# A plain first step in the first FFN, with the modulation sums divided between TensorE and VectorE

## The chip, the cores and the metric
The kernel runs on one core of one Trainium2 chip. The metric is device time of one execution in microseconds (us). A core has five engines with programs of their own: TensorE (PE in the profile), VectorE (DVE), ScalarE (ACT), GpSimd (POOL) and SyncE (SP), which here issues all DMAs. They wait for each other through semaphores only.

## The reference, cut to what matters
One layer of a streaming encoder on x of 1024 tokens by 1024 features, all in fp32: a SwiGLU FFN, a token mixer, a second FFN, each behind an RMS norm that is modulated from a vector c. The change touches the beginning of the first FFN.

```python
c_act = silu(c)
mod = c_act @ w_ada + b_ada            # 1024 x 9216, nine rows of 1024
(sh1, sc1, gt1, ...) = split(mod, 9)
h = rms_normalize(x) * (1 + sc1) + sh1
g, u = split(h @ w_ffn1_in, 2)         # 1024 x 5632
x = x + 0.5 * gt1 * (silu(g) * u) @ w_ffn1_out
```

## The kernel before, in words
**Products in three parts.** An fp32 operand is cut into a high part (rounded by ACT, `cut_hi`) and a low part (the difference, by VectorE or GpSimd, `cut_lo`). PE then does three fast matmuls, high by high, high by low and low by high, each 128x128 weights by 512 columns (L1271 to L1273).

**Halved steps.** The first FFN's input product runs in 11 steps. A step makes 512 of the 5632 columns for all 1024 tokens. It splits the inner dimension and the tokens in halves (b11, b12, b21, b22 are the quarters of the transposed h; b11 and b21 belong to the first 512 tokens, b12 and b22 to the last) and, by Winograd's form of Strassen's scheme, makes seven products instead of eight: p1 = b11, p2 = b21, p6 = t2, p7 = t3, p5 = t1, p3 = b22, p4 = t4, in this order. The t are sums of quarters: t1 = b12 - b11, t2 = b22 - t1, t3 = b22 - b12, t4 = b21 - t2. Every product exists for two groups g of weights (gate and up columns), and each of these 14 parts takes 4 x 3 = 12 matmuls, 168 a step. The weights are summed in the same manner by GpSimd (`sum1` to `sum4`), cut by ACT and GpSimd and held in a ring of seven slots, m and m + 7 in one slot. VectorE adds products from PSUM (u2, u3, c22, c12, c21), multiplies by the silu that ACT makes (a11, a22, a21, a12) and makes four sums s1 to s4 (`sums123`, `sum4`); SP stores seven operands a step for the output product.

**The start.** `Start` prepares this. SP loads pieces of w_ada for the first two rows of the modulation (8 pieces, k = 0 to 7, 1 MiB each, ring of four), the eight tiles of x (128 tokens, 0.5 MiB each, two behind each of the first four pieces), the weights of step 0 (2 MiB, ahead of the last piece) and the last piece. VectorE multiplies each piece by its 128 values of c_act and adds it to `ada_lead_acc` (L618, L621; the last in two halves, L628). PE sums the accumulator over partitions with a column of ones (L604), which gives scale and shift as columns in PSUM, half by half. Meanwhile ACT squares and scales each tile, GpSimd makes 1/rms, PE turns it (eight transposes, L596), and VectorE and ACT keep the low and the high half of it (L631, L581). Then h is modulated (b11, b21 by VectorE at L650, b12, b22 by ACT at L658), cut, and the t are made, before and during step 0. Steps 1 to 8 also carry the remaining 7 rows of the modulation: eight "rest pieces" a step, summed by VectorE into PSUM (L670, L673). A piece waits on SP for the place of the piece two before it.

**What sets the order.** All queues are written out by hand in `ffn`: one block for each engine, every engine strictly in its own order. On ACT `keep_s1` copies each p1 out of PSUM, because p2 adds on the same bank. On VectorE a step is: `hidden11`, rest 0 and 1, u2 of both groups, rest 2, u3 of both, rest 3, c22 of both, a22, rest 4, c12, a21, the three sums, rest 5, c21, a12, s4, rest 6 and 7. In step 0 the low parts of t1 and t4 stand between u2, u3 and c22.

## Time and profile before
| | us |
|---|---|
| median of 3 runs (2015.03 to 2016.78) | 2015.71 |
| profiled execution | 2015.16 |
| its span, first to last instruction | 2013.4 |
| PE busy | 1901.3 |
| VectorE, GpSimd, ACT busy | 1174.6, 893.3, 761.5 |
| mean granted TensorE clock | 0.985 |

The span is the profiler's, from the first instruction to the last; the execution's own time has 1.8 us around it. A busy PE is an engine with work in its pipe: matmuls start every 0.23 us and are shown 0.39 us long. Times of rows are counted from the span's start. Where a row of the timeline has x4, four instructions are merged and the second number is their length together.

### The profile page before, as it was taken

To read this page: it belongs to the slowest core of one execution; us is meant where nothing else is said; L and a number is where in the kernel's file an instruction comes from. 1 tells how busy PE (TensorE), PEld (TensorE's weight loads), DVE (VectorE), ACT (ScalarE), POOL (GpSimd) and SP (SyncE) were. 2 spreads that over 40 slices of the span, in tenths; PEclk is the share of its full clock that TensorE was granted. 3 is DMA by queue.
4 is the path that set the end of the run, shared out by engine and by line. 5 is a ranking of instruction groups with operands and counts; after the bars stand their busy time and mean duration, and the time that the engine had idled before them with its cause. 6 is when DMAs were issued, how large, how long until landed. Compare 5 with 4: busy or idle time off the path is not lost. (4 is left out here: it accounts for less than half of the span.)

```text
span 2013.4 us, 25362 instructions
## 1 busy us (share of the span) xinstructions
PE 1901.3 (94%) x9280; PEld 1556.2 (77%) x9280; DVE 1174.6 (58%) x1680; ACT 761.5 (38%) x1390; POOL 893.3 (44%) x642
## 2 busy tenths in 40 slices
PE   4599999999999969999999999998999999999997
PEld 3488888888888857777778887777788888888886
DVE  5867666754778780544434465559434444448777
ACT  5533222322444441444431554344323323334444
POOL 4887778766000052100012133478878778710002
PEclk9899999999999979999999999999999999999998
DMA  7155656542886301311112112433223323159652
GB/s 297 49 184 173 202 174 210 185 159 83 320 274 198 115 23 42 127 43 43 43 37 76 51 42 84 156 117 104 95 96 114 105 87 123 63 207 344 206 189 84
DMA packets 208106, 267.93 MB, mean 133 GB/s; under 512 B 14302, under 2 KB 125170, under 8 KB 206450
## 3 DMA queue, kind: packets, MB, share of 16 engines
q1 hardware_dynamic: 207986, 266.34, 39.4%
q8 instruction: 74, 1.21, 0.3%
q14 instruction: 46, 0.38, 0.1%
HBM read 211.16 MB, written 53.03 MB: 131 GB/s over the span
## 5 line engine op out<-in xcount | busy, mean ns | idle before, releaser
L420 POOL TENSOR_TENSOR ffn_ring_b<-ffn_raw_in,ffn_ring_b 128x512 fp32r<-128x512 f32 x174 | 246.8, 1424 | 144.8 <-ACT ffn_ring_b L415 144.8
L832 PE MATMUL bank<-ffn_w_hi,ffn_a_hi 128*128 128x512 f32 x616 | 240.0, 390 | 1.2 <-DVE ffn_w_lo L816 1.2
L834 PE MATMUL bank<-ffn_w_hi,ffn_a_lo 128*128 128x512 f32 x616 | 239.7, 389 | 0.0
L833 PE MATMUL bank<-ffn_w_lo,ffn_a_hi 128*128 128x512 f32 x616 | 239.7, 389 | 0.0
L1545 POOL TENSOR_TENSOR mx_w_lo<-mx_raw_w,mx_w_hi 128x1024 fp32r<-128x1024 f32 x28 | 67.5, 2420 | 364.4 <-ACT mx_w_hi L1369 297.6
L415 ACT CAST ffn_ring_b<-ffn_raw_in 128x512 fp32r<-128x512 f32 x174 | 107.9, 621 | 300.2 <-PE bank L1273 284.3
L108 POOL TENSOR_SCALAR rms<-rms 128x1 f32<-128x1 f32 x24 | 14.0, 583 | 443.8 <-ACT ffn_junk L102 430.0
L805 ACT CAST ffn_a_hi<-ffn_a_stage 128x512 fp32r<-128x512 f32 x154 | 95.6, 621 | 201.9 <-PE bank L834 197.6
L1094 DVE TENSOR_TENSOR ffn_u<-bank,ffn_u 128x512 f32<-128x512 f32 x111 | 76.4, 688 | 163.1 <-PE bank L1273 163.1
L1271 PE MATMUL bank<-h_hi,ffn_ring_a_hi 128*128 128x512 f32 x356 | 142.4, 400 | 27.8 <-ACT ffn_g L1022 18.5
L816 DVE TENSOR_TENSOR ffn_a_lo<-ffn_a_stage,ffn_a_hi 128x512 fp32r<-128x512 f32 x154 | 106.4, 691 | 74.1 <-ACT ffn_a_hi L805 74.0
L1271 PE MATMUL bank<-t_hi,ffn_ring_b 128*128 128x512 f32 x356 | 139.8, 393 | 3.3 <-DVE t_lo L287 3.3
L1272 PE MATMUL bank<-h_lo,ffn_ring_a_hi 128*128 128x512 f32 x356 | 140.5, 395 | 0.0
L1273 PE MATMUL bank<-h_hi,ffn_ring_a_lo 128*128 128x512 f32 x356 | 140.4, 394 | 0.0
L1272 PE MATMUL bank<-t_lo,ffn_ring_b 128*128 128x512 f32 x356 | 138.6, 389 | 0.0
L1273 PE MATMUL bank<-t_hi,ffn_ring_b 128*128 128x512 f32 x356 | 138.5, 389 | 0.0
L1094 DVE TENSOR_TENSOR ffn_g<-bank,ffn_g 128x512 f32<-128x512 f32 x111 | 76.3, 687 | 105.2 <-PE bank L1273 105.2
L1271 PE MATMUL bank<-h_hi,ffn_ring_b 128*128 128x512 f32 x348 | 135.5, 389 | 1.8 <-issue 1.8
L832 PEld LDWEIGHTS bank<-ffn_w_hi,ffn_a_hi 128*128 128x128 f32 x616 | 115.6, 188 | 26.8 <-DVE ffn_w_lo L816 1.5
L1273 PE MATMUL bank<-h_hi,ffn_ring_b 128*128 128x512 f32 x348 | 135.4, 389 | 0.0
L1272 PE MATMUL bank<-h_lo,ffn_ring_b 128*128 128x512 f32 x348 | 135.4, 389 | 0.0
L834 PEld LDWEIGHTS bank<-ffn_w_hi,ffn_a_lo 128*128 128x128 f32 x616 | 115.6, 188 | 24.3
(337 smaller groups left out, 4676.9 us busy)
## 6 DMA issues: line engine op xcount, KB each, us to landing
ffn_raw_in<-in_w_ffn_in SPq DMA_DIRECT2D x88, 512.0 KB, 6.0
ffn_a_stage<-hidden SPq DMA_DIRECT2D x154, 256.0 KB, 3.4
ffn_w_stage<-in_w_ffn_out SPq DMA_DIRECT2D x132, 256.0 KB, 3.1
ada_rest<-in_w_ada SPq DMA_DIRECT2D x64, 448.0 KB, 4.1
hidden<-ffn_u SPq DMA_DIRECT2D x88, 256.0 KB, 2.0
hidden<-ffn_g SPq DMA_DIRECT2D x66, 256.0 KB, 2.0
mx_raw_w<-in_w_mix_in SPq DMA_DIRECT2D x28, 512.0 KB, 3.9
ada_ring<-in_w_ada SPq DMA_DIRECT2D x8, 1024.0 KB, 12.0
```

Of the source, the lines that this page charges most:

```text
L415: act.copy(self.hi(q), self.source(b, m)).then_inc(self.hi_done, 1)
L420: pool.tensor_tensor(self.lo(q), self.source(b, m), self.hi(q).bitcast(F32), ALU.subtract)\
L805: act.copy(self.op(self.buf.a_hi, n), self.a_source(n)).then_inc(self.hi_done, 1)
L816: dve.tensor_tensor(self.op(lo, n), source, self.op(hi, n).bitcast(F32), ALU.subtract)\
L832: pe.matmul(dst, a_hi, w_hi, start=first, stop=False, skip_group_check=True)
L833: pe.matmul(dst, a_hi, w_lo, start=False, stop=False, skip_group_check=True)
L834: mm = pe.matmul(dst, a_lo, w_hi, start=False, stop=True, skip_group_check=True)
L1094: dve.tensor_tensor(dst, core.bank[:, bank_of(b, p) + g, :], src, ALU.add).then_inc(made, 1)
L1271: pe.matmul(dst, w_hi, h_hi, start=(fresh and k == 0), stop=False, skip_group_check=True)
L1272: pe.matmul(dst, w_hi, h_lo, start=False, stop=False, skip_group_check=True)
L1273: mm = pe.matmul(dst, w_lo, h_hi, start=False, stop=(k == 3), skip_group_check=True)
L1545: pool.tensor_tensor(lo, raw_w[:, slot, :], hi.bitcast(F32), ALU.subtract).then_inc(w_lo_done[slot], 1)
```

## The change
The first FFN's step 0 becomes plain. It has eight products instead of seven (k = 0 to 7 of the inner dimension, 512 tokens at a time, weights as loaded, not summed): 2 halves x 8 k x 4 column tiles x 3 = 192 matmuls. The first half needs tokens 0 to 511 alone (tiles 0 to 3). Tiles 4 to 7 are squared, scaled, turned and kept during it: PE turns tile 4 behind k = 1, tile 5 behind k = 2, tile 6 behind k = 4, tile 7 behind k = 5. The second half takes b12 and b22 themselves, whose low parts stand for that time where the high parts of t4 and t1 come later.

All parts of the first weights are cut by ACT and VectorE. GpSimd begins with the weight sums of step 1. The t operands are cut after the plain step's own, and t1, t3, t4 and the halved b22 in step 1. The results of the plain step need no sums from PSUM: silu, one multiplication each, then the sums s1 to s4.

The modulation: PE sums pieces 0 and 2 directly from the ring (each 16 matmuls of 128x128 by one column of c_act, into the banks in which it adds VectorE's accumulator at the end); VectorE sums pieces 1, 3, 4, 5, 6 and 7. The ring has six places. The order on SP is tile 0, piece 0, tile 1, piece 1, ..., tile 3, piece 3, pieces 4 to 7, the first weights, tiles 4 to 7; then, after the sums of columns, the weights of step 1, and after the last turn the rest pieces. `InWeights` counts its parts from 8 instead of 14 for step 1, and all later counts follow.

```diff
-    ADA_RING, LEAD_ACC, START_JUNK, START_XN = 32, 140, 148, 156
+    ADA_RING, LEAD_ACC, START_JUNK, START_XN = 32, 140, 203.125, 188
...
+        cut = ("t1", "t2", "t3", "t4") if by_tile else self.OPS + ("b12",)
...
+    def plain_lo(self, op, k):
+
+
+        return {"b12": self.t4_hi, "b22": self.t1_hi}[op][:, k, :] if op in ("b12", "b22") else self.lo(op, k)
...
+    def cut_plain_lo(self, dve, op, k):
+        dve.wait_ge(self.hi_done[op], k + 1)
+        dve.tensor_tensor(self.plain_lo(op, k), self.source(op, k), self.hi(op, k).bitcast(F32), ALU.subtract)\
+            .then_inc(self.plain_lo_done[op], 1)
...
+    def before(self, b):
+
+        return 0 if b == 0 else self.N * (b - self.skip) + 8 * self.skip
...
+    RING = 6
+    BY_PE, BY_DVE = (0, 2), (1, 3, 4, 5, 6, 7)
...
+        def piece(k):
             if k >= self.RING:
-                sp.wait_ge(self.summed, k - self.RING + 1)
+                self.wait_summed(sp, k - self.RING)
             sp.dma_start(self.ring[k % self.RING], self.w_ada[0, k * P:(k + 1) * P, 0:2 * D])\
                 .then_inc(self.ring_loaded[k % self.RING], 16)
-            if k < self.RING:
-                for t in (2 * k, 2 * k + 1):
-                    sp.dma_start(self.c.xres[:, t, :], self.x[0, t * P:(t + 1) * P, :])\
-                        .then_inc(self.x_loaded[t], 16)
-            if k == KD - 2:
-                first_weights()
+
+        def tile(t):
+            sp.dma_start(self.c.xres[:, t, :], self.x[0, t * P:(t + 1) * P, :]).then_inc(self.x_loaded[t], 16)
+
+        for k in range(4):
+            tile(k)
+            piece(k)
+        for k in range(4, KD):
+            piece(k)
+        first_weights()
+        for t in range(4, self.c.NS):
+            tile(t)
...
+        for t in range(6):
+            if t < 4:
+                self.square(act, t)
+            if 1 <= t <= 4:
+                self.scale(act, t - 1)
             if t >= 2:
+                self.keep_high(act, t - 2)
...
+        for t, k in enumerate(self.BY_PE):
+            pe.wait_ge(self.ring_loaded[k], 16)
             for half in range(2):
-                for k in range(4):
-                    mm = pe.transpose(c.bank[:, 4 + 2 * (t % 2) + half, k * P:(k + 1) * P],
-                                      self.xn[t % 2][:, (4 * half + k) * P:(4 * half + k + 1) * P], c.ident[:, :])
-                mm.then_inc(self.turned, 1)
+                for v in range(2):
+                    for i in range(KD // 2):
+                        r = v * KD + half * KD // 2 + i
+                        mm = pe.matmul(c.bank[:, 1 + half, r:r + 1], self.ring[k][:, r * P:(r + 1) * P],
+                                       self.c_act[:, k:k + 1], start=(t == 0 and v == 0 and i == 0),
+                                       stop=False, skip_group_check=True)
+            mm.then_inc(self.summed_by_pe, 1)
+            self.turn(pe, 2 * t)
+            self.turn(pe, 2 * t + 1)
...
+        for n, k in enumerate(self.BY_DVE):
             dve.wait_ge(self.ring_loaded[k % self.RING], 16 * (k // self.RING + 1))
             piece, c_k = self.ring[k % self.RING], self.c_act[:, k:k + 1]
-            if k == 0:
+            if n == 0:
                 dve.tensor_scalar(self.acc, piece, c_k, None, ALU.mult).then_inc(self.summed, 1)
+                self.keep_low(dve, 0)
+                self.keep_low(dve, 1)
             elif k < KD - 1:
-                dve.wait_ge(self.summed, k)
+                dve.wait_ge(self.summed, n)
                 dve.scalar_tensor_tensor(self.acc, piece, c_k, self.acc, ALU.mult, ALU.add)\
                     .then_inc(self.summed, 1)
             else:
-                dve.wait_ge(self.summed, k)
+                dve.wait_ge(self.summed, n)
                 for half in range(2):
                     part, acc = [t.rearrange("p (v d) -> p v d", v=2)[:, :, half * D // 2:(half + 1) * D // 2]
                                  for t in (piece, self.acc)]
                     dve.scalar_tensor_tensor(acc, part, c_k, acc, ALU.mult, ALU.add).then_inc(self.summed, 1)
-            for t in tiles_after.get(k, ()):
-                dve.wait_ge(self.turned, 2 * t + 1)
-                dve.tensor_copy(self.hv.tile(t, 0), self._turned_src(t, 0)).then_inc(self.kept_low, 1)
+        self.keep_low(dve, 2)
+        self.keep_low(dve, 3)
...
+class PlainStep:
+    def __init__(self, core, halved, weights, start, part):
+        self.c, self.hv, self.weights, self.start, self.part = core, halved, weights, start, part
+        self.ready, self.silu_done = core.sem("plain_ready"), core.sem("plain_silu_done")
+    def op(self, k, half):
+        return (("b11", "b12"), ("b21", "b22"))[k // 4][half]
+    def cut_hi(self, act, op, k, ready):
+        act.wait_ge(ready, k + 1)
+        act.copy(self.hv.hi(op, k), self.hv.source(op, k)).then_inc(self.hv.hi_done[op], 1)
+    def scalar(self, act, p_ready, g11_done, silu_g, at):
+        st, w = self.start, self.weights
+        C11, S1, U2, U3 = at
+        b11 = lambda k: self.cut_hi(act, "b11", k, st.h_b11)
+        b21 = lambda k: self.cut_hi(act, "b21", k, st.h_b21)
+        for m in range(4):
+            w.cut_hi(act, 0, m)
+        b11(0)
+        w.cut_hi(act, 0, 4)
+        st.square(act, 4)
+        b11(1)
+        w.cut_hi(act, 0, 5)
+        st.scale(act, 4)
+        b11(2)
+        w.cut_hi(act, 0, 6)
+        st.square(act, 5)
+        b11(3)
+        st.wait_summed(act, 4)
+        w.cut_hi(act, 0, 7)
+        st.scale(act, 5)
+        b21(0)
+        st.square(act, 6)
+        b21(1)
+        st.scale(act, 6)
+        b21(2)
+        st.square(act, 7)
+        b21(3)
+        st.scale(act, 7)
+        for half, op, made in ((0, "b12", st.h_b12), (1, "b22", st.h_b22)):
+            for k in range(4):
+                st.act_modulate(act, half, k)
+                self.cut_hi(act, op, k, made)
+        act.wait_ge(self.ready, 1)
+        act.activation(silu_g(C11), self.c.bank[:, 0, :], ACT.Silu).then_inc(g11_done, 1)
+        act.wait_ge(self.ready, 3)
+        act.activation(silu_g(S1), self.c.bank[:, 2, :], ACT.Silu).then_inc(self.silu_done, 1)
+        for m in range(3):
+            w.cut_hi(act, 1, m, p_ready)
+        self.hv.cut_hi(act, "t2")
+        act.wait_ge(p_ready, 8)
+        for bank, i in ((4, U2), (6, U3)):
+            act.activation(silu_g(i), self.c.bank[:, bank, :], ACT.Silu).then_inc(self.silu_done, 1)
+        for m in range(3, w.R):
+            w.cut_hi(act, 1, m, p_ready)
+    def vector(self, dve):
+        st, hv, w = self.start, self.hv, self.weights
+        mod = lambda k: st.dve_modulate(dve, k // 4, k % 4)
+        lo = lambda k: hv.cut_lo(dve, self.op(k, 0), ks=(k % 4,))
+        st.dve_cols(dve, 0)
+        mod(0)
+        w.cut_lo(dve, 0, 0)
+        w.cut_lo(dve, 0, 1)
+        mod(1)
+        lo(0)
+        w.cut_lo(dve, 0, 2)
+        w.cut_lo(dve, 0, 3)
+        st.dve_cols(dve, 1)
+        mod(2)
+        lo(1)
+        w.cut_lo(dve, 0, 4)
+        mod(3)
+        lo(2)
+        w.cut_lo(dve, 0, 5)
+        mod(4)
+        w.cut_lo(dve, 0, 6)
+        lo(3)
+        st.keep_both(dve, 4)
+        mod(5)
+        w.cut_lo(dve, 0, 7)
+        lo(4)
+        st.keep_both(dve, 5)
+        mod(6)
+        lo(5)
+        mod(7)
+        lo(6)
+        st.keep_both(dve, 6)
+        lo(7)
+        st.keep_both(dve, 7)
+        for k in range(4):
+            hv.cut_plain_lo(dve, "b12", k)
+            hv.make_t1(dve, st.h_b12, (k,))
+        for k in range(4):
+            hv.cut_plain_lo(dve, "b22", k)
+            hv.make_t2(dve, st.h_b22, (k,))
+    def hidden(self, dve, bank, i, dst, silu_done, n, ready, m, done):
+        dve.wait_ge(silu_done, n)
+        dve.wait_ge(ready, m)
+        dve.tensor_tensor(dst, self.c.bank[:, bank, :], self.part(0, i), ALU.mult).then_inc(done, 1)
+    def tensor(self, pe, p_ready):
+        c, hv, w, st = self.c, self.hv, self.weights, self.start
+        for half in range(2):
+            for k in range(8):
+                op = self.op(k, half)
+                if half == 0:
+                    if k == 0:
+                        pe.wait_ge(st.b_kept, 1)
+                        pe.wait_ge(st.cols_kept, 2)
+                    if k % 4 == 0:
+                        pe.wait_ge(w.lo_done, k + 4)
+                    pe.wait_ge(hv.lo_done[op], k % 4 + 1)
+                else:
+                    if k == 0:
+                        pe.wait_ge(st.kept_low, c.NS)
+                        pe.wait_ge(st.kept_high, c.NS)
+                    pe.wait_ge(hv.plain_lo_done[op], k % 4 + 1)
+                h_hi = hv.hi(op, k % 4)
+                h_lo = hv.plain_lo(op, k % 4) if half else hv.lo(op, k % 4)
+                for i in range(4):
+                    if half == 0 and k == 0 and i == 2:
+                        pe.wait_ge(st.cols_kept, 4)
+                    q = 4 * (k // 4) + i
+                    cols = slice(k % 4 * P, (k % 4 + 1) * P)
+                    w_hi, w_lo, dst = w.hi(q)[:, cols], w.lo(q)[:, cols], c.bank[:, 4 * half + i, :]
+                    pe.matmul(dst, w_hi, h_hi, start=(k == 0), stop=False, skip_group_check=True)
+                    pe.matmul(dst, w_hi, h_lo, start=False, stop=False, skip_group_check=True)
+                    mm = pe.matmul(dst, w_lo, h_hi, start=False, stop=(k == 7), skip_group_check=True)
+                    if half == 0 and k == 7:
+                        mm.then_inc(self.ready, 1)
+                    if half == 1 and k in (3, 7):
+                        mm.then_inc(p_ready, 1)
+                if half == 0 and k in (1, 2, 4, 5):
+                    st.turn(pe, {1: 4, 2: 5, 4: 6, 5: 7}[k])
...
                 start.load(sp, lambda: weights.load(sp, 0))
                 sp.wait_ge(start.cols_ready, 2)
+                weights.load(sp, 1)
+                sp.wait_ge(start.turned, 2 * NS)
             if lead:
                 lead.sync(sp)
-            weights.load(sp, 1)
+                weights.load(sp, 1)
...
+            def weight_parts(b):
                 for m in range(N):
                     if m == 2:
                         weights.sum2(pool, b)
                     if m == 4:
                         weights.sum4(pool, b)
                     weights.cut_lo(pool, b, m)
+                    if b == FIRST and start and m == 5:
+                        halved.cut_lo(pool, "t3")
+                    if b == FIRST and start and m == 7:
+                        halved.cut_lo(pool, "b22", after="t2")
+
+            if start:
+                start.pool_part(pool)
+                weights.sum13(pool, 1)
+                halved.make_t3(pool, start.h_b22)
+                weight_parts(1)
...
-                    act.wait_ge((made["a12"], c21_made)[g], (b, 2 * b)[g])
+                if b and g == 0:
+                    act.wait_ge(made["a12"], b)
+                elif b > FIRST:
+                    act.wait_ge(c21_made, 2 * (b - FIRST))
+                elif b:
+                    act.wait_ge(spilled["a12"], 16)
+                    act.wait_ge(made["s4"], 1)
...
+                start.act_lead(act)
+                plain.scalar(act, p_ready, g11_done, lambda i: part(0, i), (C11, S1, U2, U3))
...
+                start.dve_lead(dve, weights)
+                plain.vector(dve)
+                halved.make_t4(dve)
+                plain.hidden(dve, 1, C11, part(1, C11), g11_done, 1, plain.ready, 2, made["a11"])
+                plain.hidden(dve, 3, S1, part(1, S1), plain.silu_done, 1, plain.ready, 4, made["a12"])
+                halved.cut_lo(dve, "t2", after="t4")
+                plain.hidden(dve, 5, U2, part(1, U2), plain.silu_done, 2, p_ready, 6, a21_made)
+                plain.hidden(dve, 7, U3, part(1, U3), plain.silu_done, 3, p_ready, 8, made["a22"])
+                sums123(0)
+                sum4(0)
...
-                    if b == 1:
-                        dve.wait_ge(c12_made, 2)
...
-                start.pe_part(pe)
+                start.pe_lead(pe)
+                plain.tensor(pe, p_ready)
...
-        ffn1_weights = InWeights(core, "f1", buf, w_ffn1_in, InWeights.LATER)
+        ffn1_weights = InWeights(core, "f1", buf, w_ffn1_in, InWeights.LATER, plain=True)
...
```

## Rows read from the trace of the kernel before

**Rows 1.** The page, parts 1 (busy us, share, instructions) and 2 (40 slices)
```profile
PE 1901.3 (94%) x9280; PEld 1556.2 (77%) x9280; DVE 1174.6 (58%) x1680; ACT 761.5 (38%) x1390; POOL 893.3 (44%) x642
...
PE   4599999999999969999999999998999999999997
```

**Rows 2.** Waits of PE, 0 to 116 us: us in total, times, longest
```profile
PE bank L1271 <- ACT ffn_g L1022: 12.5, 1, 12.5
PE bank L1271 <- DVE h_lo L287: 8.7, 1, 8.7
PE bank L604 <- DVE ada_lead_acc L628: 8.0, 1, 8.0
...
PE bank L1271 <- DVE t_lo L287: 2.1, 3, 0.7
```

**Rows 3.** Windows: steps 1 and 2 of the first FFN (columns: us, engines, clock, DMA)
```profile
115.50:153.88 38.38, 38.36 (x170) 31.45 (x168) 23.06 (x24) 11.87 (x20) 32.09 (x24) 1.00 0.56 180
153.88:193.85 39.97, 39.97 (x184) 33.04 (x183) 25.66 (x28) 11.86 (x20) 30.33 (x23) 1.00 0.61 191
```

**Rows 4.** Timeline, opening: start us, us, engine, line, tile, [idle before <-releaser]
```profile
6.53 1.28 DVE L618 TENSOR_SCALAR ada_lead_acc<-ada_ring,c_act 128x2048 f32<-128x2048 f32 x1 [2.63 <-DMA ada_ring<-in_w_ada]
...
26.32 2.35 DVE L621 SCALAR_TENSOR_TENSOR ada_lead_acc<-ada_ring,c_act,ada_lead_acc 128x2048 f32<-128x2048 f32 x1 [1.39 <-DMA ada_ring<-in_w_ada]
...
37.28 1.66 ACT L415 CAST ffn_ring_a_hi<-ffn_raw_in 128x512 fp32r<-128x512 f32 x3 [3.64 <-DMA ffn_raw_in<-in_w_ffn_in]
...
39.71 3.49 DVE L628 SCALAR_TENSOR_TENSOR ada_lead_acc<-ada_ring,c_act,ada_lead_acc 128x1024 f32<-128x1024 f32 x2 [4.12 <-DMA ada_ring<-in_w_ada]
```

**Rows 5.** Timeline, opening: a tile's turn, the final column sum, four casts of h
```profile
11.27 1.97 PE L596 MATMUL bank<-ident,start_xn 128*128 128x128 f32 x8 [7.86 <-ACT start_xn L577]
...
41.05 6.99 PE L604 MATMUL bank<-ada_ones,ada_lead_acc 128*128 128x1 f32 x32 [8.02 <-DVE ada_lead_acc L628]
...
55.08 2.16 ACT L280 CAST h_hi<-t_raw 128x512 fp32r<-128x512 f32 x4
```

**Rows 6.** By source line, to 116 us: ns min/median/max, first and last start
```profile
L650 DVE TENSOR_SCALAR t_raw<-t_raw,mod_cols x8: 541/1482/1553, 45.0 to 65.6; 128x512 f32<-128x512 f32 x8
...
L295 DVE TENSOR_TENSOR t_raw<-h_raw,t_raw x4: 677/678/679, 60.5 to 62.3; 128x512 f32<-128x512 f32 x4
...
L287 DVE TENSOR_TENSOR t_lo<-t_raw,t_hi x12: 679/1766/1781, 82.8 to 102.1; 128x512 fp32r<-128x512 f32 x12
...
L420 POOL TENSOR_TENSOR ffn_ring_a_lo<-ffn_raw_in,ffn_ring_a_hi x7: 1270/1448/1742, 44.3 to 110.4; 128x512 fp32r<-128x512 f32 x7
```

**Rows 7.** Timeline of PE: matmuls of the first product, and of the second
```profile
57.33 0.63 PE L1272 MATMUL bank<-h_lo,ffn_ring_a_hi 128*128 128x512 f32 x1
57.75 0.63 PE L1273 MATMUL bank<-h_hi,ffn_ring_a_lo 128*128 128x512 f32 x1
...
77.94 0.63 PE L1272 MATMUL bank<-h_lo,ffn_ring_a_hi 128*128 128x512 f32 x1
...
80.92 0.63 PE L1273 MATMUL bank<-h_hi,ffn_ring_a_lo 128*128 128x512 f32 x1
```

**Rows 8.** Windows: the granted clock (third from the end) at both
```profile
56.00:58.00 2.00, 1.24 (x3) 0.83 (x3) 2.00 (x2) 1.25 (x3) 2.00 (x3) 1.00 0.06 16
...
77.00:79.00 2.00, 1.62 (x4) 1.36 (x5) 2.00 (x2) 2.00 (x5) 2.00 (x3) 0.50 0.02 4
```

**Rows 9.** Groups of ACT, 0 to 55 us: busy us, mean ns of one, idle before
```profile
L577 ACT ACTIVATE start_xn<-xres,rms 128x1024 f32<-128x1024 f32 x8 | 9.1, 1139 | 0.5 <-POOL rms L555 0.5
L571 ACT ACTIVATE start_junk<-xres 128x1024 f32<-128x1024 f32 x8 | 8.5, 1058 | 5.8 <-DMA xres<-in_x 5.7
```

**Rows 10.** Groups of VectorE, 120 to 460 us: a rest piece
```profile
L673 DVE SCALAR_TENSOR_TENSOR bank<-ada_rest,c_act,bank 128x896 f32<-128x896 f32 x48 | 55.0, 1146 | 0.8
```

**Rows 11.** Timeline of VectorE: the last sum of step 0
```profile
120.33 1.66 DVE L1140 TENSOR_TENSOR ffn_g<-ffn_u,ffn_g 128x512 f32<-128x512 f32 x1
```

**Rows 12.** The page, part 6: KB each, us to landing
```profile
ada_rest<-in_w_ada SPq DMA_DIRECT2D x64, 448.0 KB, 4.1
```

302 lines of the change are left out of this document (155 added, 147 removed).

## The prediction
> **What bounds the kernel now.** I read the page first, then PE's waits, then the opening instruction by instruction. The page has PE busy 94% of the span, and its only poor slices are the first two of 40 [rows 1]. Up to 116 us PE waits 8.0 us for VectorE's modulation sum, 8.7 us for the first low part and 12.5 us for the copy of the first product [rows 2]. From 115.50 us it never stops: step 1 has 38.36 us of PE in 38.38, step 2 39.97 in 39.97 [rows 3]. So what the change takes off the moment at which step 1 ends, 153.88 us, comes off the end. That moment is what I forecast; step 2 and all behind it keep their pace.
>
> Inside the opening three resources take turns. To about 38 us it is DMA. VectorE takes up the first piece of the modulation weights at 6.53 us, when 1 MiB has come in, and the fifth at 26.32 with 9 MiB (tiles of x included), waiting for DMA at each: 19.79 us for 8 MiB, 2.47 us per MiB from 4.1 us on [rows 4]. The FFN weights (13 MiB in) are taken up at 37.28, 1.1 us behind that line, and the last piece, which queues behind them, at 39.71 [rows 4]. Then PE sums columns for 6.99 us [rows 5], and after that ACT, VectorE and GpSimd make operands while PE is idle.
>
> **The lead.** The last piece was the 14th MiB; now it is the 10th (four tiles, eight pieces). By the line piece 1 lands at 4.1+3x2.47 = 11.5 us, piece 3 at 18.9, pieces 4 to 7 at 21.4, 23.8, 26.3 and 28.8, the weights (12 MiB) at 33.8+1.1 = 34.9, tiles 4 to 7 at 36.1 to 39.8. Both waits for a ring place are over in time (PE is done with piece 0 at 14.8, VectorE with piece 1 at 12.8, both before DMA comes to pieces 6 and 7).
> VectorE needs 2.35 us for a piece [rows 4], less than the spacing, so it ends the halves of piece 7 at 30.0 and 31.2.
> PE now also sums two pieces. The 32 records of the old final sum take 6.99 us, 0.218 each [rows 5]; a piece has as many, so 7.0 us. With turns of 1.97 us a tile [rows 5] PE's lead is 7.8 (piece 0 lands) +7 +4 +7 +4 = 29.8 us, just ahead of VectorE. The trace has no such sum beside running DMA, nor many in a row; I bound it by this row on the near side and by twice it on the far one (rival D), and take the row, the only one of that shape. The final sum gives the first columns at 30.0+3.5 = 33.5 and the second at 37.0. Before, they were there at 44.5 and 48.0.
>
> **The plain step.** It needs no sums of weights, so GpSimd's work ahead of the first product disappears. ACT casts four in 2.16 us [rows 5]: weights 0 to 3 by 37.1, the first h at 37.7. VectorE's difference lasts 0.68 us and starts every 0.60 without GpSimd beside it, against 1.77 with it [rows 6]. After the fourth cast it has one low part of h and two of weights left: first product at 39.5 us instead of 56.76. Its modulation took 0.54 to 1.55 us [rows 6]; I take 0.54, since GpSimd then does tiny norm operations alone; 1.55 for the first two, one of them behind the casts, makes it 1 us later.
> Matmuls start every 0.227 us in step 1 (168 in 38.2 without its one gap of 0.2) [rows 3]. Behind a long wait they start every 0.426 (7 in 2.98 us), the pace of 512 columns at the low level of 1.2 GHz; the granted clock was then 0.50. The first product too began 0.42 us apart, though 1.00 was shown [rows 7, 8]. About nine go at that pace, so I add 9x0.2 = 1.8 us once. 192 matmuls are 43.6 us and the four turns in between 7.9: the plain step ends at 39.5+1.8+43.6+7.9 = 92.8 us. Call it E. Its 24 matmuls more than before, 5.4 us, are contained in it.
> What feeds it is earlier: ACT has 16 casts, 4 squares (1.06+0.19) and 4 scalings (1.14) [rows 9], 18.2 us from 34.9, done at 53; VectorE, followed item by item, is 1 to 8 us ahead of PE at each k, closest at the second (40.7 against 42.2 without the slow start). It then waits for turned tiles, so these cost nothing; each microsecond of it beyond that room would be one. GpSimd's sums for step 1 lie at 52 to 59 in that slack. The last tile is kept at 67. ACT's modulate (0.8) and cast make 1.35 us per k against PE's 2.7, so the second half, from 71, does not wait either.
>
> **Step 1 pays some back.** The old step 0 had its t operands cut beside a PE that waited. Now t2, t3, b22, t1 and t4 are cut behind the second half and in step 1, and there the eight rest pieces (1.15 us each) [rows 10] fall between them. 168 matmuls are 38.1 us, so without waits step 1 would end at E+38.1.
> (1) The copy of the second p1 now waits for sum4 of step 0. VectorE from 74 (67, four k of 1.35, its own last two): eight b22 and t2 operations, four t4 (1.7 us beside GpSimd, 0.65 otherwise), two products, four t2 low parts, two more products after the silu at E+0.6, then four sums of 1.66 [rows 11]: E+10.0. PE wants that copy at E+8.2, gets it at E+10.6, so p2 ends at E+13.3.
> (2) GpSimd: from the cast at E+2 (ACT does two silu first) up to the operand of p5 it has one low part, two sums, two low parts, then t3 (four, whose casts stand behind the copy of (1), so from E+10.9), two, b22 (four), one. Eleven from E+10.9 at 1.27 to 1.74 [rows 6] end at E+24.9 to E+30.0, middle E+27.5. PE would like to start p5 at E+24.2.
> (3) VectorE from E+14.3: two rest pieces (their DMA is issued after the last store, at E+10, and takes 4.1 us) [rows 12], u2, two of t1, u2, two of t1, rest, u3, two of t4, u3, two of t4, rest, c22. Four rest are 4.6 us, five sums from PSUM 3.1, eight low parts at 1.7 13.6: E+35.6, and p3 waits for it. With p3 and p4 (10.9) step 1 ends at E+46.5. With all low parts at 0.65 it would end at E+41 by (1), at E+42 by (2). I take the contended price: 1.77 is the median of the t low parts in the old step 0 [rows 6].
> So step 1 ends at 92.8+46.5 = 139.3 us against 153.88: 14.6 less. In the old step 0 the last sums were over at 122.0 us [rows 11] and the next PE gap was only 0.2, so a VectorE that is late has no room there: I take off 0.6. Gain 14.0 us.
>
> The profiled execution took 2015.16 us around its span of 2013.4; the median is 2015.71, 0.55 more. 2015.16-14.0 = 2001.2 us.
>
> **At nothing.** The weights of step 1 are issued at 37 and needed at 80. SP waits for all turns ahead of the rest pieces, which are due after E. The store of a12 from its own place is only earlier. The tiles from 4 on arrive by 40 and are squared from 38 on in turn, one in 2.8 us.
>
> **A rule on transposes.** The turns inside the plain step are new company for matmuls. In the trace 64 transposes up to 33 us were followed by matmuls at the low pace [rows 5, 7], but the column sums and 8.7 us of idleness lie between, so it doesn't tell the two apart.
> The Trainium skill (TensorE: Matmul & The Clock Gate, "Part 4: PE-mode transpose") says that transposes do not count as busy for the clock. With idleness alone as cause the sum has one slow start; by the rule there may be one behind each turn, which is rival B.
>
> **Rivals.**
> A, no paying back (20%): the cuts fit beside the longer PE stretch; 0.68 against 1.77 speaks for it wherever GpSimd waits for ACT. Step 1 ends at E+38.1 to E+41, at 131 to 134 us: 1993 to 1996 us.
> B, PE slow in the plain step (15%): the clock falls at each of the four turns, 4x1.8 = 7.2 us, or ACT and VectorE, who hand over to each other at each k, are late by as much. For: two microseconds without a matmul four times. Against: waits of 0.7 us in the old step [rows 2] cost no more than themselves. 2008 us.
> C, a larger paying back (10%): GpSimd's lateness of 5 us at p5 (E+27.5 against the E+21.8 of a PE without waits) comes once more in step 2, if its spare 9.6 us there (39.97-30.33) [rows 3] is gone by its order of work: 2006 us.
> D, slower than before (5%): the sums on PE cost 0.43 us a record, twice the row, as nothing kept PE busy before 8 us. Then its lead ends at 43.8 and the final sum at 57.8, 20.8 us later than forecast: 2022 us. It decides from 0.36 us on (96 records, 14.0 us of gain). Against: the row's 0.218 was measured behind 8 us of idleness too [rows 2].
> The forecast itself has 50%.
>
> **How the numbers follow.** A measurement can tell about 0.2%, 4 us, from no change. Faster: the forecast, A, B and C less their tails beyond 2011.7: 88%. Within: those tails, 6%. Slower: D and a little, 6%. The range takes in A nearly whole (1993) and B with the microsecond of the modulation (2009).
>
> **What would show it.** Right: first matmul of 512 columns near 39.5; 7 us for a summed piece; last piece taken up near 29; plain step over near 93 with PE gaps below 1 us; PE waiting in step 1 about 2.4, 3 and 3 us, for the copy, a GpSimd low part and c22; step 1 over at 139, step 2 in 40. Wrong: first product after 45 (the lead), low pace between turns (B), step 1 without waits (A), waits in step 2 (C).

## The result, and the profile after

The changed kernel takes 1997.44 us (median of 4 runs, 1995.57 to 1998.71) against 2016.24 us (4 runs, 2015.03 to 2017.03): the medians are 18.8 us or 0.9% apart. The ratio estimated from all these runs is 0.9914, with a 95% interval of 0.9901 to 0.9926, so the gain is clear of the noise. The forecast was 2001.2, with a range of 1993 to 2009. The profiled execution took 1996.45 us, its span 1994.7. A second set of runs of the same kernel gave 1998.00 (4 runs, 1994.93 to 2000.77).

The page's first two parts, against [rows 1]: PE's first slices rise from 4 and 5 tenths to 7 and 9.

```profile
PE 1912.9 (96%) x9368; PEld 1571.4 (79%) x9368; DVE 1163.6 (58%) x1688; ACT 757.0 (38%) x1382; POOL 859.3 (43%) x620
...
PE   7999999999999969999999998998999999999997
```

The windows of the stages, against [rows 3] (columns as there). The plain step ends at 89.72, step 1 takes 44.50, step 2 41.45, step 3 its usual 39.93. Step 1 now begins beside unfinished operand work: its 40.0 us of busy PE hold products at the low pace, and 4.5 us are idle.

```profile
0.00:89.72 89.72, 76.69 (x353) 67.89 (x354) 59.89 (x72) 45.47 (x71) 28.39 (x37) 1.00 0.51 190
89.72:134.22 44.50, 40.01 (x170) 32.36 (x168) 36.77 (x35) 18.67 (x35) 41.93 (x29) 0.96 0.69 215
134.22:175.67 41.45, 39.93 (x183) 33.02 (x182) 27.10 (x28) 12.99 (x22) 37.32 (x28) 1.00 0.59 184
175.67:215.60 39.93, 39.90 (x183) 33.01 (x182) 25.62 (x28) 11.86 (x20) 30.29 (x23) 1.00 0.63 191
```

PE's waits from 0 to 160 us, against [rows 2]: the 12.5, 8.7 and 8.0 us are gone. The rows at lines 659, 668, 679 and 919 lie in the opening, ahead of the first product; the 3.2, 1.5 and 1.3 us at line 1502 are the paying back.

```profile
PE bank L668 <- DMA ada_ring<-in_w_ada: 4.4, 1, 4.4
PE bank L1502 <- POOL ffn_ring_a_lo L445: 3.2, 1, 3.2
PE bank L679 <- DVE ada_lead_acc L704: 3.1, 1, 3.1
PE bank L659 <- DMA b_ada_rows<-in_b_ada: 3.0, 1, 3.0
PE bank L919 <- DVE mod_cols L714: 2.5, 1, 2.5
PE bank L1502 <- ACT ffn_g L1255: 1.5, 1, 1.5
PE bank L1502 <- ACT ffn_u L1255: 1.3, 1, 1.3
```

The opening, from the timeline of all engines, against [rows 4, 5]. PE's two piece sums take 6.96 and 6.83 us. The last piece is taken up at 30.17 instead of 39.71, the final sum starts at 31.51 instead of 41.05, the first product at 40.99 instead of 56.76. The SP row at 14.77 shows pieces 6 and 7 issued only once PE has summed piece 0.

```profile
7.78 6.96 PE L668 MATMUL bank<-c_act,ada_ring 128*128 128x1 f32 x32 [4.40 <-DMA ada_ring<-in_w_ada]
...
14.77 0.80 SPq L553 DMA_DIRECT2D ada_ring<-in_w_ada  x2
...
18.05 6.83 PE L668 MATMUL bank<-c_act,ada_ring 128*128 128x1 f32 x32
...
30.17 2.48 DVE L704 SCALAR_TENSOR_TENSOR ada_lead_acc<-ada_ring,c_act,ada_lead_acc 128x1024 f32<-128x1024 f32 x2 [1.56 <-DMA ada_ring<-in_w_ada]
...
31.51 6.99 PE L679 MATMUL bank<-ada_ones,ada_lead_acc 128*128 128x1 f32 x32 [3.12 <-DVE ada_lead_acc L704]
...
40.99 0.76 PE L919 MATMUL bank<-h_hi,ffn_ring_a_hi 128*128 128x512 f32 x1 [2.49 <-DVE mod_cols L714]
```

One of the four turns inside the plain step, from PE's timeline: eight transposes between 48.05 and 48.84, and the product behind them has no low pace (0.47 us, where 0.63 is the low pace [rows 7]).

```profile
47.83 0.39 PE L921 MATMUL bank<-h_hi,ffn_ring_b 128*128 128x512 f32 x1
...
48.05 1.03 PE L651 MATMUL bank<-ident,start_xn 128*128 128x128 f32 x8
...
48.84 0.47 PE L919 MATMUL bank<-h_hi,ffn_ring_a_hi 128*128 128x512 f32 x1
```

Step 1, timeline from 113 to 124 us: PE waits 3.15 us for a GpSimd low part at p5. VectorE's c22_0 (the row at 121.27) ends at 121.95, ahead of p3 at 123.34, so that wait isn't there.

```profile
113.91 3.00 DVE L293 TENSOR_TENSOR t_lo<-t_raw,t_hi 128x512 fp32r<-128x512 f32 x2
...
114.66 1.71 POOL L445 TENSOR_TENSOR ffn_ring_a_lo<-ffn_s,ffn_ring_a_hi 128x512 fp32r<-128x512 f32 x1
...
116.42 0.79 PE L1502 MATMUL bank<-t_hi,ffn_ring_a_hi 128*128 128x512 f32 x1 [3.15 <-POOL ffn_ring_a_lo L445]
...
120.22 1.14 DVE L748 SCALAR_TENSOR_TENSOR bank<-ada_rest,c_act,bank 128x896 f32<-128x896 f32 x1
...
121.27 0.68 DVE L1322 TENSOR_TENSOR ffn_g<-bank,ffn_g 128x512 f32<-128x512 f32 x1
```

### The profile page after: what moved, and what is told of

The parts are those of the page before. It is cut to its first block and busy times, and to the rows that moved or that the text cites. A ratio compares the mean times of both kernels' runs of the same rounds, so it can differ in the third digit from the quotient of the medians.

```text
span 1994.7 us, 25490 instructions
## 1 busy us (share of the span) xinstructions
PE 1912.9 (96%) x9368; PEld 1571.4 (79%) x9368; DVE 1163.6 (58%) x1688; ACT 757.0 (38%) x1382; POOL 859.3 (43%) x620
## 5 line engine op out<-in xcount | busy, mean ns | idle before, releaser
L445 POOL TENSOR_TENSOR ffn_ring_b<-ffn_raw_in,ffn_ring_b 128x512 fp32r<-128x512 f32 x156 | 223.3, 1440 | 114.1 <-ACT ffn_ring_b L440 114.1
L440 ACT CAST ffn_ring_b<-ffn_raw_in 128x512 fp32r<-128x512 f32 x160 | 99.2, 622 | 267.4 <-PE bank L1504 255.6
L445 POOL TENSOR_TENSOR ffn_ring_a_lo<-ffn_raw_in,ffn_ring_a_hi 128x512 fp32r<-128x512 f32 x96 | 132.1, 1387 | 32.0 <-ACT ffn_ring_a_hi L440 30.0
L1502 PE MATMUL bank<-h_hi,ffn_ring_a_hi 128*128 128x512 f32 x340 | 133.7, 393 | 6.3 <-ACT ffn_g L1255 5.9
L1502 PE MATMUL bank<-h_hi,ffn_ring_b 128*128 128x512 f32 x332 | 130.3, 392 | 4.7 <-issue 1.6
L1052 PEld LDWEIGHTS bank<-ffn_w_lo,ffn_a_hi 128*128 128x128 f32 x616 | 115.6, 188 | 24.1
L1502 PE MATMUL bank<-t_hi,ffn_ring_b 128*128 128x512 f32 x340 | 133.2, 392 | 1.2 <-DVE t_lo L293 1.2
L1504 PE MATMUL bank<-h_hi,ffn_ring_a_lo 128*128 128x512 f32 x340 | 133.3, 392 | 0.0
L1503 PE MATMUL bank<-h_lo,ffn_ring_a_hi 128*128 128x512 f32 x340 | 133.2, 392 | 0.0
L1503 PE MATMUL bank<-t_lo,ffn_ring_b 128*128 128x512 f32 x340 | 132.4, 389 | 0.0
L1504 PE MATMUL bank<-t_hi,ffn_ring_b 128*128 128x512 f32 x340 | 132.3, 389 | 0.0
```

The lines of the kernel that those rows point to most:

```text
L440: act.copy(self.hi(q), self.source(b, m)).then_inc(self.hi_done, 1)
L445: pool.tensor_tensor(self.lo(q), self.source(b, m), self.hi(q).bitcast(F32), ALU.subtract)\
L1052: pe.matmul(dst, a_hi, w_lo, start=False, stop=False, skip_group_check=True)
L1502: pe.matmul(dst, w_hi, h_hi, start=(fresh and k == 0), stop=False, skip_group_check=True)
L1503: pe.matmul(dst, w_hi, h_lo, start=False, stop=False, skip_group_check=True)
L1504: mm = pe.matmul(dst, w_lo, h_hi, start=False, stop=(k == 3), skip_group_check=True)
```

## The experiments

A median of four runs of one kernel is good to about 2 us (the changed kernel's eight lie between 1994.93 and 2000.77), so causes of one to five microseconds are read from marks in the profiled run. E is the end of the plain step; M is the first column sum of the modulation's rest in step 2, and M-E tells how much step 1 and the start of step 2 pay back; M3 is the same sum in step 3, behind which every kernel runs steps of 40 us. "Before" has M3 at 205.03. The column "step 1" is the time from E to the first product of step 2 in the timeline. The kernel before was timed again beside each group of runs and did not always take the same time (third column), so medians of different groups are compared by their distance from it.

| kernel | median, us | before beside it | ratio to before, 95% | final sum | first product | E | step 1 | M-E | M3 |
|---|---|---|---|---|---|---|---|---|---|
| changed | 1997.44 | 2016.24 | 0.9901-0.9926 | 31.51 | 40.99 | 89.72 | 44.50 | 57.19 | 186.87 |
| changed again | 1998.00 | 2015.27 | 0.9890-0.9923 | 31.62 | 41.88 | 91.93 | 44.83 | 57.17 | 189.07 |
| all sums on VectorE | 1997.93 | 2016.93 | 0.9887-0.9924 | 30.33 | 39.90 | 88.64 | 44.50 | 55.99 | 184.56 |
| three pieces on PE | 1996.74 | 2015.11 | 0.9895-0.9928 | 34.80 | 43.00 | 91.86 | 44.55 | 56.03 | 187.84 |
| old order of DMAs | 2006.08 | 2016.93 | 0.9934-0.9967 | 42.44 | 50.67 | 99.36 | 44.45 | 56.01 | 195.35 |
| b22 cut late | 1996.34 | 2016.93 | 0.9886-0.9919 | 31.68 | 42.03 | 90.99 | 44.99 | 56.03 | 186.97 |
| s4 first | 1999.44 | 2016.93 | 0.9901-0.9934 | 31.56 | 41.42 | 90.86 | 43.86 | 55.30 | 186.11 |
| b22 by ScalarE | 1998.66 | 2015.11 | 0.9897-0.9931 | 31.76 | 41.71 | 90.76 | 44.97 | 55.97 | 186.69 |
| b22 by ScalarE, s4 first | 1997.95 | 2015.11 | 0.9899-0.9932 | 31.56 | 41.10 | 90.91 | 45.54 | 56.53 | 187.42 |
| rest pieces late | 2005.13 | 2015.11 | 0.9939-0.9972 | 31.54 | 41.55 | 91.16 | 45.21 | 65.07 | 196.16 |
| both lists shorter | 1993.87 | 2013.45 | 0.9881-0.9914 | 31.58 | 41.32 | 91.09 | 41.14 | 54.74 | 185.82 |
| useful ones, VectorE's list as it was | 1995.72 | 2015.27 | 0.9881-0.9914 | 30.67 | 38.90 | 88.11 | 45.50 | 56.52 | 184.55 |
| all of the useful ones | 1993.19 | 2013.45 | 0.9880-0.9913 | 30.16 | 38.39 | 87.43 | 40.39 | 53.96 | 181.37 |

The control beside the later runs:

> The changed kernel itself once more, as the control of the run beside it on the same chip. Expected: 1997.4 +-1 us, final sum at 31.5 us, first product at 41.0, plain step's end at 89.7, step 1 of 44.5 us with waits of 1.3 and 3.2 us.

It came as expected but for E, 2.2 us later: its first product started 0.9 us later, and 13 products behind it went at the low pace instead of 7. So two profiles of one kernel can differ by 2 us in E; M-E repeated to 0.02. The three kernels that change the opening alone keep the waits of step 1 and have M-E at 55.99 to 56.03, because PE's wait in step 2 is 0.3 or 0.4 us there and not 1.5 or 1.2; so 1.2 us of M-E need no cause in an edit of step 1.

### Is the division of the sums worth anything?

All eight pieces on VectorE (with it the four turns of the opening stand alone on PE, and VectorE keeps the first two tiles behind piece 2):
```diff
-    BY_PE, BY_DVE = (0, 2), (1, 3, 4, 5, 6, 7)
+    BY_PE, BY_DVE = (), (0, 1, 2, 3, 4, 5, 6, 7)
...
```


> The changed kernel with VectorE summing all eight pieces; PE only turns tiles and makes the final sum. Theory 1 (the order of the DMAs freed the lead, the division did nothing): VectorE needs 2.35 us a piece and pieces come every 2.47 us, so the final sum starts at 31.5 us as in the changed kernel and the total stays at 1997.4 within 1 us. Theory 2 (the division bought the lead): two more pieces of 2.35 us and two kept tiles before the last piece put the final sum 3 to 5 us later, and the total at 2000 to 2002.

The final sum starts 1.2 us sooner without PE's help. Its timeline shows why: VectorE waits for DMA ahead of each of the first four pieces, and works through the last four without a gap, 2.45 us apart, the pace at which they land (2.47 [rows 4]): by the landing times in the trace, 21.59, 23.99, 26.44 and 28.95 us, each is taken up within 0.1 us. PE has nothing to add. SP begins to issue pieces 6 and 7 at 9.06 us instead of 14.77, since VectorE gives piece 0's place back earlier than PE does, and the last piece is taken up at 28.98.

```profile
9.06 5.25 SPq L553 DMA_DIRECT2D ada_ring<-in_w_ada  x2
...
19.17 2.35 DVE L697 SCALAR_TENSOR_TENSOR ada_lead_acc<-ada_ring,c_act,ada_lead_acc 128x2048 f32<-128x2048 f32 x1 [0.20 <-DMA ada_ring<-in_w_ada]
...
28.98 2.48 DVE L707 SCALAR_TENSOR_TENSOR ada_lead_acc<-ada_ring,c_act,ada_lead_acc 128x1024 f32<-128x1024 f32 x2
...
30.33 6.99 PE L681 MATMUL bank<-ada_ones,ada_lead_acc 128*128 128x1 f32 x32 [7.75 <-DVE ada_lead_acc L707]
```

A dose the other way, a third piece on PE:
```diff
-    BY_PE, BY_DVE = (0, 2), (1, 3, 4, 5, 6, 7)
+    BY_PE, BY_DVE = (0, 2, 4), (1, 3, 5, 6, 7)
...
```


> Edit: TensorE sums pieces 0, 2 and 4 of the modulation, VectorE the other five (before: two and six). A dose of the division itself. Theory A: a sum on TensorE is no gain because a piece there takes 7 us at the low pace (6.83 to 6.96 measured) against 2.1 us of VectorE, and the last sum waits for the last piece to land, not for VectorE: the final sum starts at 31.5 us as before, or later where TensorE's third sum runs past the last piece (piece 4 is there at about 23 us and 7 us would end it at about 32), so the first product comes 0 to 1 us later. Theory B (VectorE's list is what binds the opening): the final sum starts 1 to 2 us sooner. If the sum of piece 4 instead takes 3.7 us, as the sum of piece 2 did in two kernels, it is hidden altogether.

The final sum is 3.3 us later than in the changed kernel and the first product 1.1 to 2.0 (more than the 0 to 1 expected): PE's third sum runs to 34.80 (theory A in kind; a piece costs VectorE 2.35 us there, not 2.1). The two doses agree: PE's 6.8 us for a piece never helps here, and hurts once PE is the later of the two. The total shows neither (1997.93, 1996.74).

```profile
28.11 6.83 PE L668 MATMUL bank<-c_act,ada_more 128*128 128x1 f32 x32
...
34.80 1.42 PE L680 MATMUL bank<-ada_ones,ada_lead_acc 128*128 128x1 f32 x6
```

### The order of the first weights

The old order of the DMAs (tiles between the pieces, the weights ahead of the last piece), all else changed:
```diff
-        for k in range(4):
-            tile(k)
...
+            if k < 4:
+                tile(2 * k)
+                tile(2 * k + 1)
+            if k == KD - 2:
+                first_weights()
...
```


> The changed kernel with the old order of the DMAs: two tiles of x behind each of the first four pieces, the first weights ahead of the last piece; all else as changed. Theory 1 (the order freed the lead): the last piece is taken up near 39.7 us instead of 30.2, the final sum starts near 41 instead of 31.5, the first product near 46 to 47 instead of 41.0, and the total is 5 to 6 us above 1997.4. Theory 2 (the division bought it): less than 2 us. In both the plain step keeps about 13 of the 18.8 us.

First product at 50.67, 9.7 us later, E 9.6 later, the time 8.6 us more. The order is a little under half of the whole gain (8.5 of 18.2 us at M3); I had expected 5 to 6 in the total. What is left with the old order is 10.9 us against the kernel before beside it, where I had expected 13. The new order with the halved step 0 was not run. The last piece is taken up at 41.10 and everything behind it moves along.

```profile
38.44 1.66 ACT L440 CAST ffn_ring_a_hi<-ffn_raw_in 128x512 fp32r<-128x512 f32 x3 [10.34 <-DMA ffn_raw_in<-in_w_ffn_in]
...
41.10 2.48 DVE L703 SCALAR_TENSOR_TENSOR ada_lead_acc<-ada_ring,c_act,ada_lead_acc 128x1024 f32<-128x1024 f32 x2 [6.24 <-DMA ada_ring<-in_w_ada]
...
42.44 6.99 PE L678 MATMUL bank<-ada_ones,ada_lead_acc 128*128 128x1 f32 x32 [14.97 <-DVE ada_lead_acc L703]
```

### Who sets the end of step 1?

GpSimd's four b22 cuts two places later in its list:
```diff
-                    if b == FIRST and start and m == 7:
+                    if b == FIRST and start and m == 9:
```


> The changed kernel with GpSimd's four low parts of b22 in step 1 behind the low part 9 of the weights instead of behind 7. Theory A (GpSimd's list alone makes PE wait at p5): the wait of 3.2 us at p5 and the slow matmuls behind it (1.3 us) go, a wait below 1 us comes at p3: 4 us less, step 2 starts at 130 instead of 134.2. Theory B (VectorE stands right behind it): its c22 is only there at 121.9 us, and PE, which would like p3 at 118.5, waits 2 to 3.5 us there, so 1 to 2 us less.

The wait of 3.15 us at p5 is gone, and one of 3.42 is at p3: step 1 takes 44.99 us, nothing less. The profile puts the wait down to a low part of GpSimd's. But of the three in the first row below, the one that p3 needs was done at 121.09 and the one that the profile names at 122.76, 0.64 us before p3; in the changed kernel p5 began 0.05 us after its low part. VectorE's c22_0 was done at 123.30, 0.10 us ahead of p3, the same distance as in the next kernels. So this is the wait of theory B, for c22:

```profile
119.38 4.62 POOL L445 TENSOR_TENSOR ffn_ring_b<-ffn_raw_in,ffn_ring_b 128x512 fp32r<-128x512 f32 x3
...
122.62 0.68 DVE L1322 TENSOR_TENSOR ffn_g<-bank,ffn_g 128x512 f32<-128x512 f32 x1
...
123.40 0.47 PE L1502 MATMUL bank<-h_hi,ffn_ring_b 128*128 128x512 f32 x1 [3.42 <-POOL ffn_ring_b L445]
```

The fourth sum ahead of the third:
```diff
+                    if fourth_early and op == "s2":
+                        dve.wait_ge(made["s2"], b + 1)
+                        sum4(b)
...
```


> The changed kernel with the fourth sum of the plain step made before the third. The copy of the second p1 waits for the fourth sum, one operation of 1.66 us earlier. Theory A (each wait in step 1 is paid on its own): the wait of 1.3 us at p2 goes, and as t3's casts stand behind the copy, GpSimd's list and the wait at p5 move with it: 1.3 to 1.6 us less. Theory B (the wait only moves, since GpSimd's list is limited by its own operations): p5 waits 1.3 us longer and nothing is gained.

The 1.34 us wait for the copy is gone, and three take its place: 0.66, 0.34 and 2.09 us (for a low part), so M-E is 55.30 against the 56.0 to 57.2 of the kernels with the same lists, and step 1 is 0.6 us shorter: between the two theories, and not seen in the time. Moving an item of either list moves the wait. Now to take items out. From GpSimd's list, b22:
```diff
-                        halved.cut_lo(pool, "b22", after="t2")
...
+        for k in range(4):
+            act.copy(self.hv.lo("b22", k), self.hv.plain_lo("b22", k).bitcast(F32)).then_inc(self.hv.lo_done["b22"], 1)
```


> Edit: the four low parts b22 that GpSimd cuts in step 1 (at product 7) are no longer cut there; ScalarE copies the plain step's own four low parts of B22, in its idle time before the end of the plain step. Theory A, GpSimd's list of some 25 us sets the end of step 1: its four cuts of b22 (about 1.3 us each) leave the list, the 3.15 us wait at 116.42 for ring_a_lo goes with the slow products behind it, and step 1 (44.5 us in the changed kernel, from the end of the plain step at 89.7) becomes about 40; the mark in step 2, 57.2 us after the plain step's end, comes at 52 to 53. Theory B, VectorE's list (c22) is nearly as late: it is next, the wait for c22_0 appears at p3 with about 1 us or more, and step 1 gets only 3 to 3.5 us shorter. Span: 3 to 5 us less than 1994.7; the total may hide 1 to 2 of it in a later change of the clock.

Theory B, and more of it than its 3 to 3.5 us allowed: nothing is gained. GpSimd starts the low part that p5 waits for 6.3 us sooner behind E (18.60 instead of 24.94), the p5 wait is gone, and PE stops at p3 for 3.44 us. Step 1 takes 44.97 us. The releaser reads "issue", but the row ahead is c22_0, done at 123.06, 0.10 us before p3:

```profile
121.32 1.14 DVE L748 SCALAR_TENSOR_TENSOR bank<-ada_rest,c_act,bank 128x896 f32<-128x896 f32 x1
122.38 0.68 DVE L1324 TENSOR_TENSOR ffn_g<-bank,ffn_g 128x512 f32<-128x512 f32 x1
...
123.16 0.47 PE L1504 MATMUL bank<-h_hi,ffn_ring_b 128*128 128x512 f32 x1 [3.44 <-issue]
```

Both edits in one kernel:

> Edit: b22's low parts of step 1 by ScalarE's copy of the plain step's, and the fourth sum of a made ahead of the third. Theory A: both waits of step 1 go, 1.34 us at its first product and 3.15 us at p5, so step 1 is 39 to 39.5 us instead of 44.5, and the mark in step 2 is 51.5 to 52 us behind the plain step's end instead of 57.2; span 1989 to 1990.5. Theory B (VectorE's list next): a wait of 1 to 2 us for c22 or hidden11 is left, and the mark is at 53 to 54.

Step 1 takes 45.54 us, M-E is 56.53, with waits of 0.99 and 4.01 us: PE arrives earlier and waits longer for the same c22. Theory B had the wait, but at 1 to 2 us. From VectorE's list, the rest pieces of step 1, all four moved behind a22:
```diff
-                    start.dve_rest(dve, b, 0)
-                    start.dve_rest(dve, b, 1)
+                    if b > FIRST:
+                        start.dve_rest(dve, b, 0)
+                        start.dve_rest(dve, b, 1)
...
+                if rest and b == FIRST:
+                    for k in range(4):
+                        start.dve_rest(dve, b, k)
```


> Edit: in step 1 alone VectorE does the four rest pieces of the modulation behind c22 and a22, not among the sums and low parts ahead of them. It tests the third step of the forecast, that these four pieces (1.15 us each, some 4.6 us of VectorE's list) delay c22 and with it p3. Theory A (GpSimd's low parts bind, VectorE's c22 is in time): c22_0 is done up to 4 us sooner, the waits of step 1 (1.34 and 3.15 us) stay within 0.3 us, step 1 stays at 44.5 us, and the time is unchanged at 1997.4 +-1.5. Theory B (as forecast): step 1 is 3 us shorter.

Both theories missed. VectorE is free for c22 at E+29.3, 2.2 us sooner, and PE's wait for GpSimd at p5 stays (3.60 us): for that part theory A holds. But the time is 7.7 us worse, though step 1 itself keeps its length (45.21): the moved pieces wait for each other's transfers (each is issued when an older one is summed), stand ahead of c12, c21 and a12, and PE pays 7.13 us in step 2. Timeline of VectorE and PE:

```profile
127.16 1.15 DVE L745 TENSOR_SCALAR bank<-ada_rest,c_act 128x896 f32<-128x896 f32 x1
...
128.43 1.15 DVE L748 SCALAR_TENSOR_TENSOR bank<-ada_rest,c_act,bank 128x896 f32<-128x896 f32 x1
...
131.69 1.16 DVE L748 SCALAR_TENSOR_TENSOR bank<-ada_rest,c_act,bank 128x896 f32<-128x896 f32 x1 [2.11 <-DMA ada_rest<-in_w_ada]
...
133.92 1.16 DVE L748 SCALAR_TENSOR_TENSOR bank<-ada_rest,c_act,bank 128x896 f32<-128x896 f32 x1 [1.08 <-DMA ada_rest<-in_w_ada]
...
149.10 0.76 PE L1506 MATMUL bank<-h_hi,ffn_ring_b 128*128 128x512 f32 x1 [7.13 <-ACT ffn_g L1255]
```

So either list alone keeps step 1 at its length: with GpSimd's shortened p3 waits for c22 until E+32.4, and with VectorE's shortened p5 waits for GpSimd until E+27.2, so that p3 begins at E+34.3. The next kernel shortens both at once. GpSimd's loses b22 as above. On VectorE's the first two rest pieces go where it is idle (3.88 us ahead of hidden11), with their loads ahead of the next weights:
```diff
+                if start and b + 1 == FIRST:
+                    start.load_rest(sp, 1, 0)
+                    start.load_rest(sp, 1, 1)
...
+                if rest and b == FIRST:
+                    start.dve_rest(dve, b, 0)
+                    start.dve_rest(dve, b, 1)
                 hidden11(b)
...
                 make_c22(b, 1)
+                if rest and b == FIRST:
+                    start.dve_rest(dve, b, 2)
+                    start.dve_rest(dve, b, 3)
...
```


> Edit: both lists of step 1 are shortened in one kernel. GpSimd's: b22's low parts by ScalarE's copy. VectorE's: rest pieces 0 and 1 of the modulation are loaded before the next weights and summed in VectorE's idle time ahead of hidden11 (it stands idle for 3.9 us there), pieces 2 and 3 behind c22_1 instead of ahead of c22_0. Shortening one list alone left the other's wait: GpSimd's alone, 3.44 us at p3 for c22; VectorE's alone, 3.60 us at p5 for a low part of a. Theory A (two lists of equal length, each enough to hold step 1): c22_0 is there at 30 us behind the plain step's end, not at 32.3, the wait at p3 falls from 3.44 to about 1 us, and the slow products behind it go too: step 1 is 2.3 to 3.6 us shorter than in the changed kernel, the mark in step 2 is 52.5 to 53.7 behind the plain step's end (56.0 to 57.2 before), and the time is 2 to 3.5 us below 1997.7. Theory B (a third thing, such as the product's clock or the weights' transfer, sets step 1): the wait moves once more, the mark stays at 56 and the time at 1997.7 +-1.5.

c22_0 is done 30.03 us behind E (32.30 with GpSimd's list alone shortened), the wait at p3 is 1.14 us, and step 1 takes 41.14 us, 3.4 to 3.7 less than in the changed kernel, where every edit of one list left 43.9 to 45.5. That is theory A. M-E is 54.74: 1.2 to 2.4 us gained rather than 2.3 to 3.6, because the copy in step 2 now holds PE for 2.44 us. The time hardly shows it: 1993.87 is 3.8 us under the middle of the changed kernel's two medians (1997.7), but the kernel before was also faster beside it. The gain over it is 19.6 us, against 18.8 and 17.3 of the changed kernel, and the intervals (0.9881 to 0.9914 and 0.9901 to 0.9926) overlap.

```profile
PE bank L1514 <- ACT ffn_g L1260: 2.4, 1, 2.4
PE bank L1514 <- ACT ffn_u L1260: 1.3, 1, 1.3
PE bank L1514 <- issue: 1.1, 1, 1.1
```

### The useful ones together

Eight sums on VectorE, the first weights in two halves along the contraction, b22 by ScalarE, s4 first; then the same with VectorE's shorter list:

> Edit: what the other experiments point to, together. All eight pieces of the modulation are summed on VectorE; the first step's weights come in two halves along the contraction, so that the first product can start on the first half; b22's low parts of step 1 by ScalarE's copy; the fourth sum ahead of the third. Theory A (each wait is gone for good): final sum at 30.3 us (1.2 less), first product at 37.5 to 39 us (2 to 3.5 less than 41.0), step 1 of 39 to 40 us instead of 44.5: 8 to 9 us less, near 1988.5 to 1989.5. Theory B (part is given back in step 2, where VectorE and GpSimd have the same lists, or at the clock's later change): 4 to 6 us less, near 1992.

> Edit: the kernel that took all eight sums on VectorE, the first weights in two halves, b22's low parts by ScalarE and the fourth sum ahead of the third (1995.7 us), with VectorE's list of step 1 shortened as in the run beside it. Theory A: first product at 38.9, plain step's end at 88.1 as there, and the mark in step 2 at 52 to 53.5 behind it instead of 56.5: 3 to 4.5 us less, 1991.2 to 1992.7. Theory B: the wait moves, 1995.7 +-1.5.

The first gave 1995.72 us (ratio 0.9881 to 0.9914), first product 38.90, E 88.11, M-E 56.52 with a 3.98 us wait at p3: the lead is gained, the step is not, and of 8 to 9 us (theory A) or 4 to 6 (B) the time shows 2.3 against the control. The second gave 1993.19 (0.9880 to 0.9913; 1989.66 to 1994.87), step 1 of 40.39 us, M-E 53.96 (theory A: 52 to 53.5) and M3 181.37, 5.5 us ahead of the changed kernel. Its gain over the kernel before beside it is 20.3 us, 1.5 to 3.0 more than the changed kernel's, which these runs cannot tell from nothing; what they show is the earlier M3.

## Why the prediction was right, and where its sizes were off

**The bound.** Right. What came off the end of step 1 came off the end: step 1 ends at 134.22 instead of 153.88, 19.7 us less; at step 3's start 18.2 are left, the medians differ by 18.8.

**The lead.** Right within 1.5 us. Piece 1 was taken up at 11.42 (forecast 11.5), piece 3 at 18.89 (18.9), the last at 30.17 (28.8), final sum 31.51 (30.0), first product 40.99 (39.5). The missing 1.2 us are the step "both waits for a ring place are over in time". SP issued pieces 6 and 7 at 14.77 us, behind PE's sum of piece 0; piece 6 still landed as forecast (26.19, 26.3), but piece 7 only at 30.15, and without that sum at 28.95. How the time of issue delays a piece that DMA reaches 11 us later is not shown. A piece on PE took 6.96 and 6.83 us (forecast 7.0), so rival D is refuted. That the sums on PE were needed at all was never asked in the forecast; the runs say they are not.

**The plain step.** The mis-sized term is the turns. I gave the four inside the step the price of the opening's, 1.97 us each, 7.9 in all; they took 0.79, 3.2 in all, 4.7 us less. The price from [rows 5] was of transposes at the low level, one every 0.21 us; inside the step they go every 0.11 (the granted clock reads 1.00 at both places, so the spacing tells). That is 0.9 us a turn. The other 0.3 are the end of the last transpose, which the next product overlaps. The slow start was 7 products, not nine (1.4 us, not 1.8). With the lead's 1.5 us the other way and 0.5 us of products above the forecast, E came at 89.72 against 92.8.

**The clock.** The first product behind each of the four turns took 0.31 us and the others ran every 0.23 us, at a granted clock of 1.00, so the clock did not fall there, and rival B is refuted. The rule of the Trainium skill that was weighed for it (TensorE: Matmul & The Clock Gate, "Part 4: PE-mode transpose") did not show in these four runs of 0.8 us, which cost no low pace behind them; no run tests it otherwise.

**Step 1.** The sum, E+46.5, was 2.0 us too much, and its three parts fared differently. (1) PE's wait for the copy: 1.34 us (forecast 2.4), since the sums were over at E+8.8, not E+10. (2) GpSimd's operand for p5 came at E+26.65 (E+27.5), the wait 3.15 us: right. (3) c22 came at E+32.2, not E+35.6: its list began 1.0 us earlier, and its eight low parts took 11.4 us by their starts and not 13.6. With that, p3, which began at E+33.6, did not wait: the step "E+35.6, and p3 waits for it" is wrong for this kernel. What ended step 1 was (2): E+26.7, three products behind it (16.3 us) and 1.3 us of low pace come to 44.3 of the measured 44.5. Yet (3) stood one place behind: as soon as p5 no longer waited, c22 was the wait, of 3.42 us with b22 cut late and 3.44 with b22 by ScalarE, and only with both lists shortened did step 1 get shorter. The stall of 3.15 us cost more than itself: six products behind it went at the low pace (granted clock 0.50 from 116.42 to 119.20 us), 2.7 us for what takes 1.4, which the forecast did not have. Behind the wait of 1.34 us there was none. PE's timeline behind the stall:

```profile
117.01 0.63 PE L1503 MATMUL bank<-t_lo,ffn_ring_a_hi 128*128 128x512 f32 x1
...
118.72 0.63 PE L1504 MATMUL bank<-t_hi,ffn_ring_a_lo 128*128 128x512 f32 x1
...
119.14 0.46 PE L1502 MATMUL bank<-t_hi,ffn_ring_a_hi 128*128 128x512 f32 x1
```

**Step 2 and the sum.** I took off 0.6 us for a late VectorE; it was 1.5 (41.45 against 39.97), a wait for the copy of p1, which was 0.3 us in three of the other kernels (all sums on VectorE, three pieces on PE, s4 first). Together: 14.0 forecast, +3.1 (E), +2.0 (step 1), -0.9 (step 2) = 18.2, the gain at step 3's start. The total came so near partly by luck: the lead and step 2 were forecast too short, the turns and step 1 too long. Rival A (no paying back) is refuted by 4.5 us of waits, though step 1's end at 134.22 lies at the edge of its 131 to 134; rival C by a step 2 without GpSimd's lateness.

What is not settled: the gain in the medians, each against the kernel before beside it, differs from the gain at M3 by up to 2.5 us either way, and by 3.4 in the last kernel (20.3 against 23.7). The granted clock in the three windows of 20 us from 1220 to 1280 us differs between the two profiles of the changed kernel (1.00, 0.91, 1.00 and 0.91, 0.99, 0.84), which fits, but no run was made to hold it.
